# Gate projection between the scan's products, and the undecayed weights by eight ScalarE copies and one addition

## What is computed

```python
def ssd_mixer(hx, hc, w_in, conv_w, conv_b, dt_bias, a_log, d_skip, norm_g, w_o, need_ctx):
    proj = jnp.concatenate([hc, hx], axis=1) @ w_in
    z, xbc, dt_raw = jnp.split(proj, [SSD_INNER, SSD_INNER + SSD_CONV_DIM], axis=-1)
    ...
    yx_f, _ = ssd_chunked(xs_x, dt_x[:, :, 0], A[0], bm_x, cm_x, hcf)
    ...
    def gate_out(y, zz):
        return rms_norm(y * jax.nn.silu(zz), norm_g) @ w_o
    out_x = gate_out(yx_f + fl(yx_b) + dsk * xs_x, z[:, Lc:])

def ssd_chunked(xs, dt, A, bm, cm, h0):
    ...
    w = cb[..., None] * decay * dtc[:, :, None]
    y_diag = jnp.einsum('bcqkgh,bckghp->bcqghp', w, xc)
    ...
    y_off = jnp.einsum('bcqgn,bcghpn,bcqgh->bcqghp', cc, h_start, jnp.exp(cum))
```

## Time and profile before

| | us |
|---|---|
| median of 3 runs (1272.42 to 1273.92) | 1272.43 |
| profiled execution, its own time | 1271.95 |
| span of that execution | 1270.2 |
| PE busy in the span | 1172.1 (92%) |
| DVE busy | 863.5 (68%) |
| ACT busy | 589.7 (46%) |
| POOL busy | 223.7 (18%) |

### The profile page before, as it was taken

How to read it: one execution, slowest core, us unless ns; L and a number is a source line. 1 busy time by engine, 2 the same in 40 slices (tenths; PEclk the granted TensorE clock), 3 DMA queues, 4 the chain that set the end, 5 groups by cost and what they waited for, 6 DMA issues and landing times.

```text
span 1270.2 us, 19422 instructions
## 1 busy us (share of the span) xinstructions
PE 1172.1 (92%) x6954; PEld 977.9 (77%) x6954; DVE 863.5 (68%) x1311; ACT 589.7 (46%) x986; POOL 223.7 (18%) x174
## 2 busy tenths in 40 slices
PE   5799999898999999999998799999888798999997
PEld 3577776688888888878888778889444697999996
DVE  0896888886887777756665778775678655555454
ACT  3657888634422232222223664455532445655542
POOL 0202444422000000000112000010787422000010
PEclk9899999999999999989999999999989798999998
DMA  9443222230765555544442142326200053665562
GB/s 380 179 134 114 84 70 81 99 135 1 244 204 183 196 198 187 176 169 160 166 135 67 44 128 70 99 67 199 67 0 1 1 166 100 199 198 182 155 184 76
DMA packets 48173, 168.19 MB, mean 132 GB/s; under 512 B 5232, under 2 KB 6512, under 8 KB 47856
## 3 DMA queue, kind: packets, MB, share of 16 engines
q1 hardware_dynamic: 48112, 167.38, 39.7%
HBM read 166.31 MB, written 1.05 MB: 132 GB/s over the span
## 4 chain that ended last, share of the span: by engine, by line
PE 77%; DVE 12%; ACT 4%; issue 3%; DMA 1%; POOL 1%; SPq 1%; DVEq 0%; ACTq 0%; POOLq 0%
PE bank L1569 23%; PE bank L1570 23%; PE bank L1571 23%; DVE w_lo L1004 2%; DVE scratch L1488 1%; DMA raw<-in_w_in 1%; PE bank L2002 1%; PE bank L2014 1%; DVE softmax_max L1175 1%; ACT w_hi L575 1%; PE bank L2024 1%; DVE scratch L1373 1%; DVE mla_h_lo L1195 1%; PE bank L2033 1%; DVE vec_weights L1081 1%
## 5 line engine op out<-in xcount | busy, mean ns | idle before, releaser
L1004 DVE TENSOR_TENSOR w_lo<-raw,w_hi 128x1024 fp32r<-128x1024 f32 (+1 forms) x226 | 270.6, 1200 | 179.8 <-ACT w_hi L575 179.6
L575 ACT ACTIVATE w_hi<-raw 128x1024 fp32r<-128x1024 f32 (+1 forms) x226 | 230.9, 1023 | 271.8 <-PE bank L1571 249.6
L1569 PE MATMUL bank<-ffn_h_lo,w_hi 128*128 128x256 f32 (+1 forms) x736 | 246.2, 335 | 8.2 <-DVE ffn_h_lo L1041 4.9
L1570 PE MATMUL bank<-ffn_h_hi,w_hi 128*128 128x256 f32 (+1 forms) x736 | 245.3, 333 | 0.0
L1571 PE MATMUL bank<-ffn_h_hi,w_lo 128*128 128x256 f32 (+1 forms) x736 | 245.3, 333 | 0.0
L1569 PEld LDWEIGHTS bank<-ffn_h_lo,w_hi 128*128 128x128 f32 x736 | 140.5, 191 | 23.8 <-issue 5.2
L1570 PEld LDWEIGHTS bank<-ffn_h_hi,w_hi 128*128 128x128 f32 x736 | 140.6, 191 | 14.5
L1571 PEld LDWEIGHTS bank<-ffn_h_hi,w_lo 128*128 128x128 f32 x736 | 140.5, 191 | 14.4
L434 POOL TENSOR_TENSOR scratch<-scratch 128x512 f32<-128x512 f32 (+1 forms) x24 | 37.4, 1559 | 602.8 <-ACT scratch L584 602.8
L1569 PE MATMUL bank<-ffn_hidden_lo,w_hi 128*128 128x256 f32 (+1 forms) x374 | 124.3, 332 | 5.7 <-DVE ffn_hidden_lo L1333 5.7
L1569 PE MATMUL bank<-ssd_h_lo,w_hi 128*128 128x256 f32 (+2 forms) x360 | 120.7, 335 | 8.0 <-DVE w_lo L1004 4.8
(11 more groups left out here) (266 smaller groups left out, 2152.8 us busy)
## 6 DMA issues: line engine op xcount, KB each, us to landing
raw<-in_w SPq DMA_DIRECT2D x120, 512.0 KB, 4.3
scratch<-in_vec_w SPq DMA_DIRECT2D x56, 512.0 KB, 3.5
vec_weights<-in_vec_w SPq DMA_DIRECT2D x24, 512.0 KB, 3.5
raw<-in_w_xbc SPq DMA_DIRECT2D x24, 512.0 KB, 3.4
ada_start<-in_ada_w SPq DMA_DIRECT2D x8, 1024.0 KB, 17.4
raw<-in_w_z SPq DMA_DIRECT2D x16, 512.0 KB, 3.5
raw<-in_w_so SPq DMA_DIRECT2D x16, 512.0 KB, 4.3
raw<-in_w SPq DMA_DIRECT2D x16, 384.0 KB, 3.8
```

What stands on the lines that cost most here:

```text
L575: A(wh[s % RING][:, 0:c], raw[s % RING][:, 0:c], ACT.Copy).then_inc(w_hi, 1)
L1004: V.tensor_tensor(wl[s % RING][:, 0:c], raw[s % RING][:, 0:c], wh[s % RING][:, 0:c].bitcast(f32), SUB).then_inc(w_lo, 1)
L1569: mm(o, lh, rl, start=first, stop=False)
L1570: mm(o, lh, rh, start=False, stop=False)
```

## The change

PE now computes four gate tiles ahead of the scan and the other twelve within it: in turns 0 to 5, `z_tile(4 + 2m)` stands behind `decay(m+2, 0)` and `z_tile(5 + 2m)` behind `decay(m+2, 1)`, ahead of `to_features(m)`. Tiles 4 to 15 go to bank 5; `to_features` shares bank 4 with `diagonal`. ACT copies each tile out without the SiLU (`z_out`, with the same `hi(ZS + t + 4)` behind it), and applies the SiLU in place to four tiles at once (`z_silu`). DVE's `lo` of those blocks stand singly between the instructions of the scan. The masks and the weights W lie in the context columns of `ssd_h`, which the gate tiles do not read, so `mask_forward(0)` waits only for the convolution's tiles (`w_used` at `ZS`). The forward part of the undecayed weights is now made by eight ACT copies with a factor (`forward`), and DVE adds both parts with one instruction of 1024 columns.

```diff
             def mask_forward(m):
...
+            pool.wait_ge(w_used, ZS)
+            pool.wait_ge(dt_dve, 12)
+            mask_forward(0)
             pool.wait_ge(w6_done, 3)
             pool.wait_ge(conv_ev, 20)
-            pool.wait_ge(dt_dve, 12)
+            weigh_x(0)
             pool.wait_ge(cb_done, 4)
             backward(0)
-            weigh_x(0)
-            pool.wait_ge(w_used, SO)
-            mask_forward(0)
             weigh_x(1)
+            mask_forward(1)
             backward(1)
-            mask_forward(1)
...
-            with act.Fori(0, 4) as i:
-                for u in range(4):
-                    act.wait_ge(w_used, ZS + 4 * i + u + 1)
-                    A(zs[:, ds(4 * i + u, 1), :].rearrange("p o t -> p (o t)"), bank[4 + u % 2][:, 0:LAT], ACT.Silu).then_inc(conv_y, 1)
-                    hi(ZS + 4 * i + u + 4, ZS + u + 4)
+            def z_out(t):
+                act.wait_ge(w_used, ZS + t + 1)
+                A(zs[:, t, :], bank[z_bank(t)][:, 0:LAT], ACT.Copy).then_inc(z_cp, 1)
+                hi(ZS + t + 4, ZS + t + 4)
+
+            def z_silu(g):
+                act.wait_ge(z_cp, 4 * g + 4)
+                z = zs[:, 4 * g:4 * g + 4, :]
+                A(z, z, ACT.Silu).then_inc(z_done, 1)
+            def forward(m):
+                g, c = divmod(m, 2)
+                if m >= 1:
+                    act.wait_ge(wf, m)
+                for h in range(GH):
+                    q = slice(128 * (h % 4), 128 * (h % 4) + 128)
+                    last = A(T[:, 2 + h // 4, q], cbf[:, 4 * c + g, :], ACT.Copy, scale=dt[:, 2 + c, GH * g + h:GH * g + h + 1])
+                last.then_inc(gf, 1)
...
+            z_out(0)
+            z_out(1)
             act.wait_ge(dt_dve, 12)
             mask_backward(0)
+            z_out(2)
+            z_out(3)
+            act.wait_ge(cb_done, 4)
+            forward(0)
+            z_silu(0)
             start_state(0)
             exps(0)
             mask_backward(1)
             start_state(1)
+            forward(1)
             exps(1)
             mask_backward(2)
             for m in range(8):
                 if m < 6:
                     start_state(m + 2)
+                    forward(m + 2)
+                    z_out(4 + 2 * m)
                     exps(m + 2)
+                    z_out(5 + 2 * m)
                 if m < 5:
                     mask_backward(m + 3)
+                if m in (1, 3, 5):
+                    z_silu((m + 1) // 2)
...
                 dve.wait_ge(gb, m + 1)
-                if m >= 1:
-                    dve.wait_ge(wf, m)
-                for h in range(GH):
-                    q = slice(128 * (h % 4), 128 * (h % 4) + 128)
-                    last = V.scalar_tensor_tensor(T[:, 2 + h // 4, q], cbf[:, 4 * c + g, :], dt[:, 2 + c, GH * g + h:GH * g + h + 1],
-                                                  T[:, 4 + h // 4, q], MUL, ADD)
-                last.then_inc(gd, 1)
+                dve.wait_ge(gf, m + 1)
+                V.tensor_tensor(T[:, 2:4, :], T[:, 2:4, :], T[:, 4:6, :], ADD).then_inc(gd, 1)
...
+            lo(ZS + 4, ZS + 4)
+            lo(ZS + 5, ZS + 5)
             undecayed(0)
-            with dve.Fori(0, 4) as i:
-                for u in range(4):
-                    lo(ZS + 4 * i + u + 4, ZS + u + 4)
             states(0)
             decayed(0)
             carried(0)
+            lo(ZS + 6, ZS + 6)
+            lo(ZS + 7, ZS + 7)
             states(1)
             undecayed(1)
             carried(1)
...
                 if m < 6:
+                    lo(ZS + 8 + 2 * m, ZS + 8 + 2 * m)
                     states(m + 2)
                     undecayed(m + 2)
+                    lo(ZS + 9 + 2 * m, ZS + 9 + 2 * m)
                 add_diagonal(m)
                 gate(m)
...
                 if m < 6:
                     states(m + 2)
                     decay(m + 2, 0)
+                    z_tile(4 + 2 * m)
                 diagonal(m)
                 if m < 6:
                     decay(m + 2, 1)
+                    z_tile(5 + 2 * m)
                 to_features(m)
                 if m < 6:
                     carried(m + 2)
```

More of the change, by code:

```diff
@@ L134, with z_bank @@
 ADD1, ADD2, ADD3, ADD4 = 11, 20, 28, 36
+def z_bank(t):
+    return 4 + t % 2 if t < 4 else 5
 STATE_TILES = (((0, 0), (1, 2), (2, 4)), ((0, 1), (1, 3), (3, 5)))
@@ L229, in program @@
             with ExitStack() as ph2:
+                hf = sb("h_space", [128, 2 * KD, TOK], f32, ph2)
                 xs2 = sb("xs", [128, 3, GW], f32, ph2)
[L231 to L236 removed]
                 hst = sb("state", [128, 2, 2, GW], f32, ph2)
[L238 to L241, removed]
             with ExitStack() as ph2:
@@ L252, in program, with squared, mask_at, weights_at @@
             w6 = sb("state_w", [128, 6, SH], f32, ph)
+            E = sb("decay", [128, GH, 128], f32, ph)
+            Y = sb("y_tok", [128, 4, GW], f32, ph)
+            def squared(g):
+                return xtok[:, 2:4, GW * g:GW * g + GW]
+            xsf = (T[:, 0, :], T[:, 1, :], tab[:, TAB["cos"]:NTAB], xs2[:, 0, :], xs2[:, 1, :], xs2[:, 2, :])
+            def mask_at(d_):
+                return hf[:, 0:KD, 128 * d_:128 * d_ + 128]
+            def weights_at(u):
+                return hf[:, KD:2 * KD, 128 * u:128 * u + 128]
         with ExitStack() as ph:
@@ L291, in program @@
         st_cp, st_dec, st_sum, off_mm = (sem(x) for x in ("st_copied", "st_dec", "st_sum", "off_mm"))
-        mk_f, mk_b, dec_mm, dec_exp, gb, gd, wf = (sem(x) for x in (
-            "masked_forward", "masked_backward", "dec_mm", "dec_exp", "g_backward", "g_done", "w_f32"))
+        mk_f, mk_b, gf, dec_mm, dec_exp, gb, gd, wf = (sem(x) for x in (
+            "masked_forward", "masked_backward", "g_forward", "dec_mm", "dec_exp", "g_backward", "g_done", "w_f32"))
+        z_cp, z_done = sem("z_copied"), sem("z_done")
         off_rd, y_off = sem("off_read"), sem("y_off_done")
@@ L931, in mask_backward @@
                     at = 32 + GH * g + h
-                    last = A(mk[:, 1, h, :], tabv("ge"), ACT.Copy, scale=dtA[:, 2 + c, at:at + 1])
+                    last = A(mask_at(1)[:, h, :], tabv("ge"), ACT.Copy, scale=dtA[:, 2 + c, at:at + 1])
                 last.then_inc(mk_b, 1)
+            def forward(m):
[6 more added lines that the diff above has]
+                last.then_inc(gf, 1)
             def start_state(e):
@@ L1973, in _, with z_tile @@
                 last.then_inc(cb_mm, 1)
-            def z_tile(t, u):
-                tile(ZS + t, ZS + u, bank[4 + u % 2][:, 0:LAT], lambda k: H1h[:, k, CTX:TOK],
+            def z_tile(t):
+                if t >= 2:
+                    pe.wait_ge(z_cp, t - 1 if t < 4 else t)
+                tile(ZS + t, ZS + t, bank[z_bank(t)][:, 0:LAT], lambda k: H1h[:, k, CTX:TOK],
                      lambda k: H1l[:, k, CTX:TOK], 0, 8, True, True).then_inc(w_used, 1)
-            z_tile(0, 0)
+            z_tile(0)
             to_tokens(22, 0, 18)
             to_tokens(23, 1, 19)
[L1982 to L1989, removed]
+            for t in range(1, 4):
+                z_tile(t)
             def decay(m, d_):
@@ L2001, in decay @@
                 for b in range(2):
-                    last = mm(bank[6 + b][:, :], tabv(("gt", "lt")[d_]), mk[:, d_, 4 * b:4 * b + 4, :].rearrange("p h q -> p (h q)"),
+                    last = mm(bank[6 + b][:, :], tabv(("gt", "lt")[d_]), mask_at(d_)[:, 4 * b:4 * b + 4, :],
                               start=d_ == 0, stop=d_ == 1)
@@ L2029, in diagonal @@
                 if m:
-                    pe.wait_ge(y_done, m)
+                    pe.wait_ge(yt_done, m)
+                else:
+                    pe.wait_ge(z_cp, 3)
                 for h in range(GH):
                     xs = slice(64 * h, 64 * h + 64)
-                    last = mm(bank[4][:, xs], W[:, m % 2, h, :], xtok[:, 2 + c, GW * g + 64 * h:GW * g + 64 * h + 64], start=True, stop=True)
+                    last = mm(bank[4][:, xs], weights_at(m % 2)[:, h, :], xtok[:, 2 + c, GW * g + 64 * h:GW * g + 64 * h + 64], start=True, stop=True)
                 last.then_inc(dg_mm, 1)
@@ L2038, in to_features @@
                 pe.wait_ge(y_done, m + 1)
-                if m:
-                    pe.wait_ge(yt_done, m)
                 for f in range(4):
-                    last = nc.tensor.transpose(bank[5][:, 128 * f:128 * f + 128], Y[:, 2 * (g % 2) + c, 128 * f:128 * f + 128], tabv("ident"))
+                    last = nc.tensor.transpose(bank[4][:, 128 * f:128 * f + 128], Y[:, 2 * (g % 2) + c, 128 * f:128 * f + 128], tabv("ident"))
                 last.then_inc(yt_mm, 1)
```

7 lines of the change are left out of this document (4 added, 3 removed).

## The result

| | before | changed |
|---|---|---|
| median, us | 1272.99 (4 runs, 1272.42 to 1273.92) | 1295.3 (4 runs, 1290.21 to 1297.31) |
| ratio to before | | 1.0168, 95% interval 1.0137 to 1.02 |
| again, on a further chip | 1272.79 (9 runs) | 1293.84 (5 runs), ratio 1.0169, 1.0155 to 1.0183 |
| profiled execution | 1271.95 | 1297.31 |

A forecast was written before the change was run, and what follows sets the result against it. It took PE to bound the gate stage and no engine alone the scan. Terms -39.5 + 2.0 + 2.5 + 1.0 + 54.2 gave +20.2 us on the profiled 1271.95, so 1292 us, range 1278 to 1299.

The forecast's parts named there:

- gate stage gone: Ahead of the scan: its first product starts when tile 3 ends, 856.2 instead of 895.65, taking away 39.5 us.
- prologue: From the scan's first product to carried(1): more ACT work ahead of the first start_state makes it 2.0 us longer.
- `decay(2, 0)` waits for POOL: At decay(2, 0), PE waits for POOL's third mask: +2.5 us, and +1.0 for half of a clock fall.
- six turns: work 15.6, wait, clock: Turns 0 to 5: each 15.6 us PE work, 3.9 wait, 2.2 clock; six take 130.2 against 76, +54.2 us.
- The added wait: Ahead of to_features each turn: PE idles 3.9 us while ACT copies and makes w_hi, DVE makes w_lo and adds the diagonal.
- this rule: For w_lo beside POOL: the later of two such SBUF instructions fully blocks, adding 0.3 to 1 us per turn, 2 to 6 in all.
- The clock: Behind each turn's idle time, PE's low clock costs 2.2 us, between 0 and 3.2.
- rival B: In the turns: the wait comes, the clock stays, 19.1 to 20.5 us a turn, 1280 us in total; chance 0.17.
- C: In the turns: wait 4.3 and clock 3.2 at their upper ends, 23.1 us a turn, 1301 us in total; chance 0.10.
- The 2.8 us of drain: In the prologue: by the skill's 1.38 us drain per switch, two table switches would add up to 2.8 us; not in the sum.
- The shorter undecayed: On DVE in the turns: 1.23 to 2.1 us for 2.2 to 4.5, ahead of DVE's new wait, so it gives nothing.
- Rival A: In the turns: PE is the bound, tiles fill its idle time, clock stays up, 15.6 us a turn, 1252 us; chance 0.08.

The follow-up runs named there:

- the fillers: Changed kernel plus useless PE products, unread by anything, in the wait ahead of to_features in turns 0 to 5: 1282.55 us, ratio 1.0081 to the kernel before.
- the run with one line moved: Changed kernel with the w_lo of block ZS+9+2m on DVE behind carried(m+2) instead of ahead of add_diagonal(m): 1259.88 us, ratio 0.9903 to the kernel before.
- the run with the mask later: One-line-moved kernel, plus w_lo of block ZS+8+2m behind undecayed(m+2) and POOL's first mask_forward waiting for the convolution's last copies: 1257.63 us, ratio 0.9884.
- four more moves: Changed kernel with both w_lo and POOL's first mask later, and the last gate tile moved from turn 5 to turn 6: 1254.3 us, ratio 0.9856.
- the second part alone: Kernel before plus only ACT's forward copies and DVE's single addition, undecayed(0) behind the gate's w_lo loop, gate tiles ahead of the scan: 1264.1 us, ratio 0.9927.
- POOL held back: Changed kernel where POOL, in turns 0 to 4, starts backward and mask_forward only after w_lo of block ZS+9+2m: 1287.48 us, ratio 1.0116 to the kernel before.

## Why the prediction was right

Forecast 1292 (1278 to 1299), measured 1295.3 and 1293.8. By its steps, in the profiled execution:

| step | forecast | measured |
|---|---|---|
| gate stage gone | -39.5 | -38.5 |
| prologue | +2.0 | +1.4 |
| `decay(2, 0)` waits for POOL | +2.5, clock +1.0 | +1.3, clock 0 |
| six turns: work 15.6, wait, clock | 3.9 + 2.2, 21.7 a turn | 4.2 + 2.4, 22.2 a turn |
| tail | 0 | +0.5 |
| sum | +20.2 | +22.3 |

How the right column comes about: the scan's first product stands 55.4 us behind the start of the stretch before (895.65 - 840.28) and 16.9 after (859.76 - 842.91). The prologue takes 16.9 us after for 15.5. The turns run from 876.67, the start of `states(2)`, to 1011.01, that of `diagonal(6)`, 134.3 us; without the 1.3 for POOL that is 133.0, six of 22.2, where before they took 75.4. The six waits add up to 25.2 us, 4.2 each, and 133.0 - 93.6 - 25.2 = 14.2 is left for the clock, 2.4 each. Some 0.2 of that is not the clock's: with the fillers, at full clock, a turn takes 20.15 us, where 15.63 and a wait of 4.3 make 19.9.

Part of the closeness is luck: gate stage, turns and tail came out 4.9 us longer than forecast and the prologue with `decay(2, 0)` 2.8 shorter.

**The added wait** is the step that decides, and the run with one line moved shows it: with it 22.2 us a turn, without it 15.6, and 16.9 in two of them. I had put it at 3.9 between 3.5 and 4.3. In turns 1 to 4 it was at the upper end, 4.3, because POOL's mask runs beside this `w_lo`; the first (4.67, `w_lo` 2.63) and the last (3.27, `w_lo` 1.22, no mask) lie outside. The order in which they start decides who pays: `w_lo` ends 1.07 us after the POOL instruction (918.28 against 917.21), nearly its own 1.23. That is what the Trainium skill says ("SBUF — State Buffer", Who interferes with whom): the ports that VectorE shares with GpSimd are an exclusive lock, and the order of issue decides who blocks. The prediction set this rule apart and had it add 0.3 to 1 us a turn; in turns 1 to 4 it was 0.4 over my 3.9, so the rule was the better guide.

**The clock** was forecast at 2.2 and the fillers show 2.0, so rival B (the clock stays up) is out. C put both at their ends: the wait nearly got there, the clock did not. My two prices for it were a little high. I set the transposes' 1.12 and 0.65 us against 0.44, which is a set that follows other work; behind a wait at full clock the same chain shows 0.66. So the fall after 3.40 us cost 2.9 and not 3.2, and the one after 2.71 cost 1.7 and not 1.9. The 2.2 between 0 and 3.2 was a choice, not worked out.

**The prologue** was forecast too long by 2.8 us in all. `decay(2, 0)` waited 1.3 us, short of 1.5 to 3.5, and no clock fell there. The 2.8 us of drain that the prediction kept apart for two table loads did not show: in the prologue the next ACT instruction stands 0.01 to 0.02 us behind either load.

**What the sum left out** is that POOL's early mask would meet the last convolution taps on DVE (3.11 us for 1.65); the -39.5 lost 1.0 us by it. I named POOL's mask as free to start and did not look at who works then. The run with the mask later shows that the 1.0 comes back in the prologue, so as a whole it cost nothing.

**The shorter undecayed** "gives nothing": it gave less than nothing, -1 us on DVE and by that +1 us on the wait, since POOL started earlier. This was not foreseen.

**Rival A** asked for `w_lo` to be ready before the tile ends. Its 1252 us were reached but for 2, not by the change but with four more moves, and with its 15.6 us a turn.

The profiled executions differ by 25.4 us and not 22.3, mostly because the stretch begins 2.6 us later in one. PE's work ahead of it is the same in both kernels, and in the eleven profiled executions of this study it began anywhere from 836.25 to 842.91. That is also the reason to measure the touched stretch and not the span.

## What to carry to other kernels

When work that needs no other engine is put into an engine's idle time, follow the steps that prepare its operands: here the gate tiles were free for PE, but the ring of four tied a weight block to the tile just done, and the instruction that made it stood on DVE ahead of the one for which PE waited. In an engine's queue a step that nobody needs for a turn belongs behind the one that somebody waits for now; that one line was worth 34 us. An edit that also moves another instruction tests both: 3.3 of the 9 us of the second part alone came from such a move. And before a sum is made of idle times, look at which other instructions start in them, since a shorter or an earlier one can start a third engine at a worse moment.

## What the runs showed of the hardware

- VectorE and GpSimd, both on two operands in SBUF: the instruction that starts first takes its usual time, the other is held up by about what is left of it. `w_lo` took 2.26 us for 1.23 when POOL's mask had started 0.71 us earlier, and the mask took 2.88 for 1.90 when `w_lo` had started 0.23 us earlier. Where no mask ran, in turn 5 and with POOL held back, `w_lo` took 1.22 to 1.23.
- TensorE's clock: idle times of 3.3 to 4.7 us in each turn brought the mean granted clock to 0.89. Useless products that left 0.5 us of idle on either side (0.9 once) kept it at 1.00 and made the kernel 11 us faster with more work. Idle times of the same length did not always lower it: 3.28 us did not in turn 0 of the run with POOL held back, 3.27 did in turn 1; 3.01 did not the earlier trace rows and 2.71 did in the kernel before.
- A table load on ACT takes 1.28 us and the next instruction starts 0.01 to 0.02 us behind it unless it waits for PE, in the changed kernel too; the move of the gate tiles splits them over the turns, with four loads for SiLU as before and three for the exponentials where one stood, and no wait of PE in turns 0 to 5 came to stand behind one.
